# Attention units in pairs: masks first, one run of score products, one run of weighted sums, one compressed join per head pair

## The reference, cut to what matters

```python
for l in range(DEPTH):                       # 2
    proj = x @ w_in[l]                       # (512, IN_WIDTH)
    y_ssm, y_pool = s5_mixer(...), pool_mixer(...)
    # attention: 8 heads of 64, 2 kv heads, 512 tokens
    p_cmp = masked_softmax(q @ kc.T * scale, cmp_mask)   # 31 compressed blocks
    out = g0 * (p_cmp @ vc)                              # compressed branch
    # n_top is all 8 blocks, window 512 = the whole sequence: both branches are causal attention
    for n, (k, v) in enumerate(((k_sel, v_sel), (k_win, v_win))):
        out += g[n + 1] * (masked_softmax(q @ k.T * scale, causal) @ v)
    x = layer_norm(ALPHA * x + merged(y_ssm, y_pool, out) @ w_out[l]); x = layer_norm(ALPHA * x + ffn(x))
```

## Time and profile before

| | |
|---|---|
| median of 3 runs | 1764.71 us (1764.57 to 1766.1) |
| span of the profiled execution | 1767.2 us |
| PE busy | 1733.0 us, 98% |
| DVE busy | 944.0 us, 53% |
| ACT busy | 649.2 us, 37% |
| PE waits for `gates` in the attention stage | 2.7 us (layer 0), 2.4 us (layer 1) |

### The profile page before, as it was taken

The page is one execution under the profiler, slowest core; times in us unless marked ns, Lnnn a source line. Parts: engine busy times, 40 slices in busy tenths (PEclk is TensorE's granted clock), DMA queues, the critical chain, the costliest instruction groups (busy, mean ns, idle before and its releaser), DMA issues.

```text
span 1767.2 us, 26801 instructions
## 1 busy us (share of the span) xinstructions
PE 1733.0 (98%) x10172; PEld 1409.5 (80%) x10172; DVE 944.0 (53%) x1514; ACT 649.2 (37%) x1152; POOL 125.6 (7%) x252
## 2 busy tenths in 40 slices
PE   7999999999999999999999999999999999999998
PEld 6778777788888888888888777777888888888886
DVE  5788778444354444422358877775453544444223
ACT  4333666422252222221353346664222522222112
POOL 4700000000000000000037000000000000000000
PEclk9999999999999999999999999999999999999999
DMA  7443111133513222222263431112233222222222
GB/s 259 157 117 88 53 50 49 49 101 102 169 63 105 95 95 95 95 96 95 91 244 110 116 86 50 53 37 72 96 119 119 82 98 95 95 95 95 96 96 83
DMA packets 65918, 174.88 MB, mean 99 GB/s; under 512 B 14256, under 2 KB 26576, under 8 KB 65056
## 3 DMA queue, kind: packets, MB, share of 16 engines
q1 hardware_dynamic: 40192, 140.53, 24.5%
q10 hardware_dynamic: 21888, 13.64, 3.2%
q0 software_dynamic: 3744, 19.41, 3.2%
HBM read 162.27 MB, written 7.08 MB: 96 GB/s over the span
## 4 chain that ended last, share of the span: by engine, by line
PE 86%; DVE 7%; DVEq 3%; ACT 2%; issue 1%; DMA 0%; ACTq 0%
PE ps L532 19%; PE ps L534 18%; PE ps L533 18%; PE ps L572 6%; PE ps L570 6%; PE ps L571 6%; PE ps L857 2%; PE ps L844 2%; PE ps L830 1%; DVE wlo L1376 1%; PE ps L550 1%; PE ps L561 1%; PE ps L552 1%; PE ps L551 1%; PE ps L583 1%
## 5 line engine op out<-in xcount | busy, mean ns | idle before, releaser
L532 PE MATMUL ps<-xh,whi 128*128 128x512 f32 x1312 | 520.0, 396 | 8.4 <-ACT gates L1190 5.1
L534 PE MATMUL ps<-xh,wlo 128*128 128x512 f32 x1312 | 511.3, 390 | 0.0
L533 PE MATMUL ps<-xl,whi 128*128 128x512 f32 x1312 | 510.9, 389 | 0.0
L1376 DVE TENSOR_TENSOR wlo<-raw,whi 128x1024 fp32r<-128x1024 f32 x264 | 324.9, 1231 | 347.4 <-ACT whi L977 338.2
L977 ACT ACTIVATE whi<-raw 128x1024 fp32r<-128x1024 f32 x264 | 278.9, 1057 | 351.0 <-PE ps L572 234.3
L532 PEld LDWEIGHTS ps<-xh,whi 128*128 128x128 f32 x1312 | 246.4, 188 | 61.4 <-issue 7.8
L534 PEld LDWEIGHTS ps<-xh,wlo 128*128 128x128 f32 x1312 | 246.3, 188 | 52.3
L533 PEld LDWEIGHTS ps<-xl,whi 128*128 128x128 f32 x1312 | 246.6, 188 | 48.8 <-issue 0.5
L570 PE MATMUL ps<-whi,hh 128*128 128x512 f32 x352 | 137.5, 391 | 0.0
L572 PE MATMUL ps<-whi,hl 128*128 128x512 f32 x352 | 137.0, 389 | 0.0
L571 PE MATMUL ps<-wlo,hh 128*128 128x512 f32 x352 | 137.0, 389 | 0.0
(11 more groups left out here) (338 smaller groups left out, 2335.5 us busy)
## 6 DMA issues: line engine op xcount, KB each, us to landing
raw<-wstream SPq DMA_DIRECT2D x264, 512.0 KB, 3.3
w<-w1s POOLq DMA_DIRECT2D x4, 2048.0 KB, 11.7
sm<-smalls POOLq DMA_DIRECT2D x2, 1060.0 KB, 6.7
xt<-xin ACTq DMA_DIRECT2D x4, 512.0 KB, 6.3
scratch_u<-pa ACTq DMA_DIRECT2D x8, 256.0 KB
toep<-scratch_k ACTq DMA_DIRECT2D x4, 512.0 KB
toep_b<-scratch_k ACTq DMA_DIRECT2D x4, 512.0 KB
xt<-xin POOLq DMA_DIRECT2D x4, 512.0 KB, 4.0
```

Of the source, the lines that this page charges most:

```text
L532: pe.matmul(ps[:, bank, :], wh, hi[:, k, :], start=first and i == 0, stop=False)
L533: pe.matmul(ps[:, bank, :], wh, lo[:, k, :], start=False, stop=False)
L534: m = pe.matmul(ps[:, bank, :], wl, hi[:, k, :], start=False, stop=last and i == len(blocks) - 1)
L1376: dve.tensor_tensor(wlo[:, c % 2, :], raw[:, c % 2, :], whi[:, c % 2, :].bitcast(f32), SUB).then_inc(lo_ready, 1)
```

## The change

Units are handled two at a time, `i` and `i + 1` with `i` even, on all three engines.

- PE: `masks` for both units come ahead of `scores(i + 2)` and `scores(i + 3)`, which then accumulate onto them. Per pair: `turned(i)`, the four masks, both scores, filler(i), `turned(i + 1)`, filler(i + 1), `weighted(i)`, `weighted(i + 1)`.
- PE: the compressed branch is one product over all 512 columns, at u = 7.
- ACT and DVE: both units' `max_part` and `exps` stand together, ahead of `scale(i + 2)`; the gate's or the query's write-out (`filler_out`) comes after them. `ysh` follows the pair's second `turned_first` and `scale(i + 3)`. `gelu_in` is at the end of the pair u = 0, 1, `gelu_low`, `rope` and `query_parts` at the end of u = 2, 3.

The diff, cut to its core:

```diff
+                def masks(i):
+                    t = i % 8 // 2
+                    for kv in range(2):
+                        pe.matmul(ps[:, sbank(i) + kv, P * t:P * t + P], identb[:, :], dmaskb[:, :], start=True, stop=True)
...
                 def scores(i):
...
-                            pe.matmul(ps[:, sbank(i) + kv, 0:n], a[rows, P * t:P * t + P], b[rows, br, 0:n],
-                                      start=a is qh and b is krh, stop=False)
-                    for kv in range(2):
-                        m = pe.matmul(ps[:, sbank(i) + kv, P * t:n], identb[:, :], dmaskb[:, :], start=False, stop=True)
+                            m = pe.matmul(ps[:, sbank(i) + kv, 0:n], a[rows, P * t:P * t + P], b[rows, br, 0:n],
+                                          start=False, stop=b is krl, skip_group_check=True)
...
-                    if i % 8 == 3:
+                    if i % 8 == 7:
                         pe.wait_ge(cs_tready, l * 4 + (j + 1))
-                    if br and t:
-                        for t2 in range(t) if t == 1 else ():
-                            pe.matmul(ps[:, 7, P * t2:P * t2 + P], vct[:, :], pct[:, P * t2:P * t2 + P], start=False, stop=False)
-                        m = pe.matmul(ps[:, 7, P * t:P * t + P], vct[:, :], pct[:, P * t:P * t + P], start=False, stop=i % 8 == 7)
-                    if i % 8 == 7:
-                        m.then_inc(o_psum, 1)
+                        pe.matmul(ps[:, 7, :], vct[:, :], pct[:, :], start=False, stop=True).then_inc(o_psum, 1)
...
+                for i in range(0, 32, 2):
+                    j, u = i // 8, i % 8
+                    if u == 4:
+                        pe.wait_ge(cs_tready, l * 4 + (j + 1))
                     turned(i)
...
                     if i < 30:
+                        pe.wait_ge(s_exp, l * 32 + (i + 2))
+                        masks(i + 2)
+                        masks(i + 3)
                         scores(i + 2)
+                        scores(i + 3)
...
+                    filler(i)
...
+                    pe.wait_ge(pt_first, l * 32 + (i + 1))
+                    if u > 3:
+                        pe.wait_ge(pt_second, l * 16 + (4 * j + (u - 3)))
+                    turned(i + 1)
...
+                    filler(i + 1)
...
                     weighted(i)
+                    weighted(i + 1)
```

ACT and DVE, the new loops:

```diff
+                for i in range(0, 32, 2):
+                    turned_first(i)
+                    if u == 0 and j:
+                        heads_out(j - 1)
...
+                    next_split(i)
+                    if i < 30:
+                        exps(i + 2)
+                        exps(i + 3)
+                    if u == 0 and j:
+                        compressed_exp(j)
+                    if i < 30:
+                        scale(i + 2)
+                    filler_out(i)
+                    if u == 2:
+                        act.wait_ge(cs_tpsum, b + 1)
+                        act.activation(pct[:, :], ps[0:2 * NP, 3, :], ACT.Copy).then_inc(cs_tready, 1)
+                    turned_first(i + 1)
...
+                    next_split(i + 1)
+                    if i < 30:
+                        scale(i + 3)
+                    if u == 2:
...
+                        act.activation(ysh[:, j, :].rearrange("p (n t) -> p n t", t=TAP), ygt[:, :].rearrange("p (t n) -> p n t", n=NCH), ACT.Copy, scale=0.5)\
+                    filler_out(i + 1)
+                    if u == 0:
...
+                        act.activation(ygt[:, :], ygt[:, :], ACT.Tanh, scale=GELU_B).then_inc(gelu_tanh, 1)
+                for i in range(0, 32, 2):
+                    turned_second(i)
+                    if u == 0 and j:
+                        heads_low(j - 1)
+                    if i < 30:
+                        max_part(i + 2)
+                        max_part(i + 3)
+                    next_lo(i)
+                    if u == 0 and j:
+                        compressed_in(j, 3)
+                        compressed_shift(j)
+                    if i < 30:
+                        scale(i + 2)
+                    if u == 2:
+                        gelu_out(j)
+                    if u == 0 and j:
+                        compressed_scale(j)
+                    pool_pass(j, u)
+                    turned_second(i + 1)
+                    next_lo(i + 1)
+                    if i < 30:
+                        scale(i + 3)
+                    if u == 0:
+                        gelu_in(j)
+                    if u == 2:
+                        gelu_low(j)
+                        if j < 3:
+                            rope(j + 1)
+                            query_parts(j + 1)
+                    pool_pass(j, u + 1)
```

More of the change, by code:

```diff
@@ L880, in _ @@
                 compressed_scores(0, 3)
+                masks(0)
                 scores(0)
@@ L883, in _ @@
                 pe.wait_ge(x_state_taken, l * 4 + 4)
+                masks(1)
                 scores(1)
@@ L894, in mix, with filler @@
                     pe.matmul(ps[:, mix_bank(g), :], smv("wpool", 4, P)[:, g, :], pla[:, g, :], start=True, stop=True).then_inc(mix_psum, 1)
-                for i in range(32):
+                def filler(i):
                     j, u = i // 8, i % 8
+                    if j < 3 or u < 6:
+                        at, k0, k1 = unit_part(j, u)
+                        part_slab(first_slab(j) + at, k0, k1)
+                    else:
+                        mix(2 * u - 12)
+                        mix(2 * u - 11)
+                for i in range(0, 32, 2):
+                    j, u = i // 8, i % 8
+                    if u == 4:
+                        pe.wait_ge(cs_tready, l * 4 + (j + 1))
                     turned(i)
@@ L909, in _ @@
                         s5_outputs(l * 4 + 3, 3)
[L910 to L921 removed]
+                    filler(i)
+                    if u == 2:
+                        pe.wait_ge(cs_ready, l * 4 + (j + 1))
+                        if j == 0:
+                            pe.wait_ge(yfm_in, l * 4 + 4)
+                        compressed_turned(j)
+                    pe.wait_ge(pt_first, l * 32 + (i + 1))
+                    if u > 3:
+                        pe.wait_ge(pt_second, l * 16 + (4 * j + (u - 3)))
+                    turned(i + 1)
+                    if i == 0:
+                        s5_back(l * 4 + 3, 3)
+                    filler(i + 1)
                     if i == 0:
@@ L1268, in heads_out, with turned_first @@
                     act.activation(nsh[:, j, :], ps[:, 7, :], ACT.Copy).then_inc(o_hi, 1)
[L1270 to L1274, removed]
-                def mix_hi(g):
-                    act.wait_ge(mix_psum, l * 4 + (g + 1))
-                    act.activation(plh[:, g, :], ps[:, mix_bank(g), :], ACT.Copy, scale=smv("psc")[:, g:g + 1]).then_inc(mix_hi_ready, 1)
-                for i in range(32):
-                    j, u = i // 8, i % 8
-                    b = l * 4 + j
+                def turned_first(i):
+                    u = i % 8
+                    w = P * (u // 2 + 1)
                     act.wait_ge(s_tpsum, l * 32 + (i + 1))
-                    w = P * (u // 2 + 1)
                     if u < 4:
@@ L1846, in _ @@
                 scale(0)
+                scale(1)
                 compressed_scale(0)
@@ L1868, in mix_low, with turned_second @@
                        .then_inc(mix_ready, 1)
-                for i in range(32):
-                    j, u = i // 8, i % 8
-                    at, k0, k1 = unit_part(j, u)
+                def turned_second(i):
+                    u = i % 8
                     if u > 3:
@@ L1875, in _, with next_lo, pool_pass @@
                         dve.tensor_copy(probt[:, i % 2, 1, 0:P * (u // 2 + 1)], ps[:, 3, 0:P * (u // 2 + 1)]).then_inc(pt_second, 1)
-                    if i < 31:
-                        scale(i + 1)
-                    if u == 0 and j:
-                        heads_low(j - 1)
-                    if i < 30:
-                        max_part(i + 2)
-                    if u == 0 and j:
-                        compressed_in(j, 3)
-                        compressed_shift(j)
+                def next_lo(i):
+                    j, u = i // 8, i % 8
+                    at, k0, k1 = unit_part(j, u)
                     if k0 == 0 and at < 3:
                         split_lo(hl_, first_slab(j) + at + 1)
-                    if u == 1:
-                        if j:
-                            compressed_scale(j)
-                        gelu_in(j)
-                    if u == 2:
-                        gelu_out(j)
-                    if u == 3:
-                        gelu_low(j)
-                    if u == 3 and j < 3:
-                        rope(j + 1)
-                        query_parts(j + 1)
+                def pool_pass(j, u):
                     if j == 0 and u > 3:
```

56 lines of the change are left out of this document (29 added, 27 removed).

## The result

| | before | after |
|---|---|---|
| median of 4 runs | 1764.64 us (1763.43 to 1766.1) | 1788.81 us (1786.93 to 1790.05) |
| ratio of the times | 1 | 1.0130, 95% interval 1.0118 to 1.0142 |
| span of the profiled execution | 1767.2 us | 1785.1 us |
| mean granted clock of that execution | 0.997 | 0.988 |
| attention stage, layer 0 and 1, first transposes to the first slab behind it | 158.8, 158.5 us | 168.6, 168.9 us |

The change makes the kernel 1.3% slower, as forecast, and 4.8 us more than the forecast of 1784.

A forecast was written before the change was run, and what follows sets the result against it. PE, busy for 98% of the span, was taken as the bound. The median 1764.7 us, less 23.5 of gains (15 + 3.4 + 5.1), plus 34 of new waits and 9 of clock, gave 1784 us; range 1755 to 1796.

The forecast's parts named there:

- PE's own time: On PE, seams and masks per pair of units fall from 1.56 to 1.09 us: 0.47 saved, 15 us over 32 pairs.
- The upper bound of 22: On PE, at most 0.7 us saved per pair, with no entry cost left at slab and transposes: 22 us.
- The drain at a switch of tile shape: On PE, if each switch drains TensorE, 128 removed switches save at least 0.08 us more each, 10 us in all.
- The join: On PE, three visits to the compressed join become one per head pair: 0.42 us saved each, 3.4 us in all.
- Waits that go: PE's old waits on ACT's gate write all vanish: 2.7 us and about the same in the other layer, 5.1 us.
- The DVE late: At u=4 to u=5 of each j=0 to 2, the DVE reaches unit 4's copy late, at j=1 at 23.1 us.
- The waits: At u=5, PE waits 4.4 us for gates (j=0 to 2) and for transposes 1.85 (0.3 at j=0): 34 us.
- The clock: Behind the gate waits the clock falls at six places, 1.5 us lost each (bounds 0 and 1.7): 9 us.
- The sum: Whole kernel: median 1764.7 us plus 10.5 net of waits and gains, plus 9 for the clock, gives 1784 us.
- A DVE in time: Rival: the DVE reaches unit 4's copy early, gate waits are 2.4 us per place, time 1756 us; chance 0.16.
- the switches save nothing, 1799: Rival: on PE, seams between masks, scores and slab cost what the removed ones did, 15 us more; chance 0.08.
- The two rivals without a fallen clock, 1775 and 1768: Late DVE with full clock, 1775 us, chance 0.14; full clock plus 7 us more switch saving, 1768, chance 0.08.

The follow-up runs named there:

- x2_seam_ysh: Changed kernel with slabs cut so that none begins inside a pair, and ACT's ysh right behind pct, ahead of unit 3's copy: 1757.43 us, ratio 0.9942.
- x9_filler_first: x8_join_thrice with the slab part of u=6 ahead of the masks of units 8 and 9, in j=0 to 2: 1746.45 us, ratio 0.9886.
- b1_seam: Kernel before with only the slabs cut anew (second slab units 2 and 3, third 4 to 7), units one by one: 1762.91 us, ratio 0.9981.
- x7_pe_seam: x6_pe_only with the slabs cut anew (second slab units 2 and 3, third 4 to 7): 1756.93 us, ratio 0.9951.
- b2_join: Kernel before with only the compressed join made one product over 512 columns at u=7: 1766.38 us, ratio 1.0000.
- x8_join_thrice: x7_pe_seam with the compressed join block by block at u=3, 5 and 7 again: 1751.59 us, ratio 0.9918.
- x4_rope_late: Changed kernel with rope and query_parts moved to the u=4 pair, behind the maxima and the scale: 1766.48 us, ratio 0.9997.
- x3_gate_mid: Changed kernel with ACT's gate write-out of u=4 between the exponentials of units 6 and 7: 1771.83 us, ratio 1.0029.
- x6_pe_only: Changed kernel's order on PE, with ACT's and the DVE's order and the slab cut of the kernel before: 1764.09 us, ratio 0.9985.
- x5_copy_early: x2_seam_ysh with the DVE's copy of u=5 right behind the two maxima and the pool sum last: 1754.97 us, ratio 0.9936.

## Why the prediction was right, step by step

- **PE's own time: right in kind, 0.13 per pair too small.** Where nothing waits (x2_seam_ysh, then x9_filler_first), parts of the pair u=4, 5 of j=1 read:

```profile
233.78 0.82 PE L848 MATMUL ps<-cn,prob 128*128 128x128 f32 x6
234.35 0.47 PE L532 MATMUL ps<-xh,whi 128*128 128x512 f32 x1
...
235.91 0.88 PE L861 MATMUL ps<-probt,vtok 128*64 128x128 f32 x12
```

```profile
235.27 1.55 PE L861 MATMUL ps<-probt,vtok 128*64 128x128 f32 x24
236.75 0.48 PE L868 MATMUL ps<-pct,vct 64*128 64x128 f32 x2
```

  Start to start: transposes 0.71 and masks 0.31 (233.49, 234.20 and 234.51 in the profile after), scores 1.58, first slab part 1.49 (232.29 to 233.78 in x2_seam_ysh), second transposes 0.57, second slab part 1.56, weighted sums 1.48. The sum is 7.70 against 8.30 before: 0.60 saved, where the prediction had 0.47. The term that was mis-sized is the second transposes: 0.57 where it had 0.71. That is less than the 0.65 of its six transposes at 0.109 each, so a run of transposes between two slab parts shows no price to get in and out. The head pairs say the same: 37.92 in b1_seam and 35.5 in x9_filler_first, both without waits and with the join in three visits, 2.4 for four pairs. Over 32 pairs it is 19 us, not 15. The upper bound of 22 was not reached.
- **The drain at a switch of tile shape.** The masks, scores and weighted sums take what the rows of the kernel before had said, to 0.04, and the extra 0.13 is at transposes between slab parts, where the tile shape doesn't switch. The Trainium skill (TensorEngine Tiling (Array Packing), Key Properties) says that changing the tiling mode drains TensorE, and gives no price. The prediction's estimate from it, 0.08 more for each of four removed switches per pair, makes 0.79 in all; the measured 0.60 does not bear that out.
- **The join: right on PE, no gain by itself.** One visit takes 1.05 (248.98 to 250.03 in x7_pe_seam) against 1.48 for three: 0.42 less, as predicted. In the sum it may stand, since the waits were worked out with it gone from u=3 and u=5. But from "all visits are on PE's chain" I expected 3.4 us from this part alone, and that failed: in six of eight head pairs a wait took the gain back (b2_join), or more (x8_join_thrice against x7_pe_seam).
- **Waits that go.** At j=3 the wait of 1.0 us went: the head pair is 3.7 us shorter (predicted 3.3). Less 0.42 for the join and 1.0 for the wait, that leaves 0.57 for each of its four pairs, near the 0.60.
- **The DVE late: right nearly to the tenth.** After the first transposes of j=1 (215.56), predicted and read: ysh ends 18.8 and 18.8; query_parts 23.1 and 23.1; transposes of u=5 start at 23.75 and 23.7; the slab runs at 28.85 and 28.8. That this lateness makes the transposes wait, and 1.6 of the 4.24 us of the gates, x4_rope_late shows. That `ysh` is about 1 us of it, x2_seam_ysh shows with the seam gone; moving `ysh` alone in the changed kernel was not tried.
- **The waits.** From when PE could have gone, the gates cost 4.52 us (239.24 + 0.57 to 244.33; 4.4 predicted), and the transposes 1.66 (236.09 + 1.49 to 239.24; 1.85 predicted). The brackets say 4.24 and 1.49: an idle time is counted from the modelled end of the last product, while an unhindered successor starts before that end (in the earlier trace rows at 236.07, where the row before it ends at 236.15). Six times 4.5 are 27; the transposes, with 3.6 and 3.3 in the brackets and 0.17 more for each, make 8; the small waits at L861 make 1.
- **The clock: right that it falls at all six, but 1.5 us a place was too small.** The bound of 1.7 came from the earlier trace rows, where the low clock lasted one short stretch. Behind the wait at 240 to 244 PE was busy for 1.67 + 2.00 us at 0.50 and 2.00 at 0.89, so 0.84 + 1.00 + 0.22 = 2.1 us were lost. Worked out in this way j=0 lost about 1.6, j=2 about 2.3; six places make 12, not 9.
- **The sum.** 27 + 8 + 1 + 12 = 48 lost, against 19 for PE, 3.4 for the join and 5 for the old waits, 27: +21. The two stages read +9.8 and +10.4, 20.2 in all. The forecast's +19.5 was thus near by errors that cancel: 4 us too little saved, against 3 us too little for the clock and 2 for the waits. It is not exact either: the medians lie 24.2 us apart and the profiled spans 17.9. Spans are 1.8 us shorter than times, so the profiled execution of before lies 4.4 us above its median, and that of after, the shortest of its four, 1.9 below: these make the 6.3. The profiled execution of before had two falls of the clock outside the stages (at 514 and 886 us), that of after one, which is 1.7 of the 4.4; the rest stays open. For the 1.9, the other three executions of after had a mean clock of 0.985 to 0.987 instead of 0.988, so they spent more time at the low clock; where, no profile of them shows.
- **The rivals.** A DVE in time was tried and doesn't win as the kernel stands (x4_rope_late): the clock falls all the same. That the switches save nothing, 1799, is excluded by 0.60 per pair. The two rivals without a fallen clock, 1775 and 1768, are excluded by the six falls.

## What to carry to other kernels

Merging runs on the busiest engine saves what its seams cost, and that can be read from start to start in one unit (here 0.60 us of 8.30); but each seam also held the work that covered another engine's write-out, so list for every wait what stands between the two, before and after. Where two units go together on the busy engine, the slower engines need not be merged in the same way, and here it cost: put each write-out or copy that the busy engine needs next ahead of the second unit's work, not behind it (x3_gate_mid, x6_pe_only). Moving work later on a helper engine (`ysh`, 1.1 us) delays the queue of a third engine by about its length at each place (5.4 us of waits over six places), and here the clock doubled that. Each gap of 4.5 us on TensorE cost some 2 us more in clock.

## What the runs showed of the hardware

The length of a wait alone did not tell whether the clock would fall. In x7_pe_seam the same wait of 1.44 us for the same instruction (the masks at u=6) left the clock alone in j=1 and was followed by 1.2 GHz in j=2 (as in j=0):

```profile
240.00:242.00 2.00, 0.67 (x7) 0.43 (x4) 1.85 (x5) 1.49 (x5) 0.00 (x0) 1.00 0.01 2
242.00:244.00 2.00, 1.89 (x19) 1.66 (x20) 1.70 (x5) 1.68 (x5) 0.00 (x0) 1.00 0.00 0
```

```profile
278.00:280.00 2.00, 0.72 (x10) 0.64 (x12) 1.77 (x6) 2.00 (x6) 0.00 (x0) 0.99 0.00 0
280.00:282.00 2.00, 2.00 (x13) 1.69 (x12) 1.67 (x7) 1.14 (x5) 0.00 (x0) 0.50 0.03 8
```

And in x5_copy_early a wait of 1.93 us, with PE busy for 0.15 of 2 us, left it at full speed, and so did one of 2.23 us at j=2:

```profile
236.00:238.00 2.00, 0.15 (x4) 0.00 (x0) 1.66 (x7) 1.75 (x6) 0.00 (x0) 1.00 0.15 23
238.00:240.00 2.00, 1.92 (x24) 1.74 (x24) 1.83 (x5) 0.64 (x2) 0.00 (x0) 1.00 0.61 240
```

The Trainium skill (TensorE: Matmul & The Clock Gate, HAM oscillation) describes a matmul loop in which every long wait puts the array back to half rate. The six waits of over 4 us agree. That section does not say that shorter waits can do it, and here those of 1.44 to 2.7 us did so at some places and not at others. What decides it is not shown.
